# A two-block transformer kernel: SWA heads and MLA heads in one pipeline of single heads, gates as tanh

## The reference

```python
h = rmsnorm_2(x, mix_norm_g)
proj = h @ w_in          # 1024 x (512+128+128+384+256+32+1024+1024)
qa, ka, va, q_lat, kv_lat, k_r, g_a, g_b = split(proj)
qa, ka = rope(qa), rope(ka)                      # 8 query heads, 2 key heads of 64
o_a = swa_sink_attention(qa, ka, va, sinks)      # window of 128, a sink in the sum
cq = rmsnorm_2(q_lat, q_norm_g); qb = cq @ w_uq  # 384 -> 8 heads of 64+32
ckv = rmsnorm_2(kv_lat, kv_norm_g); kvb = ckv @ w_ukv   # 256 -> 8 x (64+64)
o_b = mla_attention(q_nope, rope(q_rope), k_nope, rope(k_r), vb)  # 8 causal heads
y = sigmoid(g_a) * (o_a @ w_o_swa) + sigmoid(g_b) * (o_b @ w_o_mla)
x = x + y @ w_out
```

## Time and profile before

| | |
|---|---|
| median of three runs | 1207.67 us |
| the profiled execution | 1208.16 us |
| its span, first to last instruction | 1206.3 us |
| PE busy / DVE busy / ACT busy | 1152.8 / 693.5 / 577.8 us |
| second mixer, from its second input piece to the first product with `w_out` | 823.9 to 984.9 us |
| PE clock in slices 31 and 33 of 40 | 0.9 |
| PE clock in slice 32 | 0.6 |

### The profile page before, as it was taken

The page is one execution under the profiler, slowest core; times in us unless marked ns, Lnnn a source line. Parts: engine busy times, 40 slices in busy tenths (PEclk is TensorE's granted clock), DMA queues, the critical chain, the costliest instruction groups (busy, mean ns, idle before and its releaser), DMA issues. The chain is left out here.

```text
span 1206.3 us, 14165 instructions
## 1 busy us (share of the span) xinstructions
PE 1152.8 (96%) x5890; PEld 968.2 (80%) x5890; DVE 693.5 (57%) x779; ACT 577.8 (48%) x821; POOL 28.6 (2%) x34
## 2 busy tenths in 40 slices
PE   5999999999999999999999999999999889999997
PEld 4888887999989977777778888878887677888886
DVE  4654545667666667777466445455756266654443
ACT  4533345445455455654355433455556344534343
POOL 0000000000011200000000000000000000000000
PEclk9999999899999999999999999999999699999999
DMA  9565554555543335345456665654633234665650
GB/s 316 193 202 179 189 195 144 179 175 175 177 138 115 131 105 192 108 139 190 140 176 207 190 194 178 202 166 142 198 118 104 70 105 158 200 201 174 195 189 35
DMA packets 129967, 198.59 MB, mean 165 GB/s; under 512 B 5584, under 2 KB 98640, under 8 KB 129648
## 3 DMA queue, kind: packets, MB, share of 16 engines
q1 hardware_dynamic: 128272, 190.75, 48.8%
q0 software_dynamic: 1632, 6.95, 1.5%
HBM read 196.63 MB, written 1.05 MB: 164 GB/s over the span
## 5 line engine op out<-in xcount | busy, mean ns | idle before, releaser
L889 DVE TENSOR_TENSOR WL<-RAW,WH 128x2048 fp32r<-128x2048 f32 (+1 forms) x181 | 405.7, 2264 | 104.3 <-ACT WH L429 104.1
L429 ACT ACTIVATE WH<-RAW 128x2048 fp32r<-128x2048 f32 (+1 forms) x181 | 338.3, 1890 | 18.8 <-DMA RAW<-in_w_in 9.4
L1435 PE MATMUL PS<-WH,XTH 128*128 128x512 f32 (+1 forms) x700 | 277.3, 396 | 1.4 <-ACT V L616 0.9
L1437 PE MATMUL PS<-WH,XTL 128*128 128x512 f32 (+1 forms) x700 | 273.1, 390 | 0.0
L1436 PE MATMUL PS<-WL,XTH 128*128 128x512 f32 (+1 forms) x700 | 272.4, 389 | 0.0
L1435 PE MATMUL ACC<-WH,KTH 128*128 128x512 f32 (+1 forms) x466 | 186.6, 400 | 9.3 <-DVE KTL L978 6.0
L1437 PE MATMUL ACC<-WH,KTL 128*128 128x512 f32 (+1 forms) x466 | 183.8, 395 | 0.0
L1436 PE MATMUL ACC<-WL,KTH 128*128 128x512 f32 (+1 forms) x466 | 183.7, 394 | 0.0
L1435 PEld LDWEIGHTS PS<-WH,XTH 128*128 128x128 f32 x700 | 131.5, 188 | 27.8 <-ACT V L616 1.4
L1437 PEld LDWEIGHTS PS<-WH,XTL 128*128 128x128 f32 x700 | 131.4, 188 | 27.9
L1436 PEld LDWEIGHTS PS<-WL,XTH 128*128 128x128 f32 x700 | 131.6, 188 | 25.8
(11 more groups left out here) (258 smaller groups left out, 1322.0 us busy)
## 6 DMA issues: line engine op xcount, KB each, us to landing
RAW<-in_w_in SPq DMA_DIRECT2D x48, 1024.0 KB, 5.2
RAW<-in_ffn_w_gate SPq DMA_DIRECT2D x44, 512.0 KB, 4.0
RAW<-in_ffn_w_up SPq DMA_DIRECT2D x44, 512.0 KB, 5.0
RAW<-in_ffn_w_down SPq DMA_DIRECT2D x22, 1024.0 KB, 4.9
RAW<-in_w_gate SPq DMA_DIRECT2D x22, 512.0 KB, 3.9
RAW<-in_w_up SPq DMA_DIRECT2D x22, 512.0 KB, 4.9
RAW<-in_w_down SPq DMA_DIRECT2D x11, 1024.0 KB, 4.9
RAW<-in_ssd_w_branch SPq DMA_DIRECT2D x8, 1024.0 KB, 5.0
```

Source lines behind the costliest of these rows:

```text
L429: nc.scalar.activation(WH[:, s, 0:n], RAW[:, s, 0:n], ACT.Copy).then_inc(w_hi, 1)
L889: tt(WL[:, s, 0:n], RAW[:, s, 0:n], WH[:, s, 0:n].bitcast(F32), ALU.subtract).then_inc(w_lo, 1)
L1435: mm(ps, stat_hi, mov_hi, start=first, stop=False)
L1437: return mm(ps, stat_lo, mov_hi, start=False, stop=last)
```

## The change

Only the second mixer changes.

- The input projection's pieces are cut otherwise (`IN2_COLS`): first the query latent and the SWA keys (512 columns), then the SWA queries (512), then SWA values, the KV latent and the rope key (416).
- The order of units is new: `U_UQ` at once after the projection, the gate chunks `U_G2` between and behind `U_UKV` and `U_OSWA`.
- The 16 heads (8 SWA, then 8 MLA) go singly through a loop of 18 steps. In step q PE computes the scores of head q, a `cover(q)`, the products with V of head q-2, the transposes of the probabilities of head q-1, and in steps 7 to 14 the four transposes of MLA head q-7. Scores have one PSUM bank (4), turned probabilities one (5), products with V one (6).
- A cover is a piece for one tile of 128 tokens: 12 matmuls of 512 columns in most steps, 24 in steps 0, 1, 10, 11 and 12. All gate chunks, `U_UKV`, the whole SWA branch (steps 11 and 12) and the first piece of the MLA branch (step 17) are covers.
- The gates are kept as tanh of half the logit, straight from PSUM (ACT's `g2_keep`). The merges compute (tanh + 1) times product in one instruction, and `kt_hi` and `kt_lo` of the product with `w_out` carry a factor 0.5. The sigmoid passes (L790) and their table load are gone; a load of the table set with exp and tanh is added ahead of the heads.

The core of the diff:

```diff
-            for q in range(1, 3):
-                banks = (in2_bank(q, 0), in2_bank(q, 1))
...
-            first_half(g2_unit(0), (0, 1), lambda t: pe.wait_ge(proj_kept, t + 3))
...
+            def head_scores(q):
+                r = q % SWA_HEADS
+                if q:
+                    pe.wait_ge(s2_ready, q)
+                if q < SWA_HEADS:
...
+                else:
+                    pe.wait_ge(mla_kept, r + 1)
+                    qt, kt = QK[0:MLA_QK, r, 0, :], QK[0:MLA_QK, r, 1, :]
+                mm(PS[4][:, 0:P], qt[:, 0:P], kt[:, 0:P], start=True, stop=True)
+                mm(PS[4][:, P:3 * P], qt[:, P:TOK], kt[:, :], start=True, stop=True).then_inc(sc2, 1)
+            def head_turn(q):
+                pe.wait_ge(p2_exp, q + 1)
+                if q:
+                    pe.wait_ge(p2_kept, q)
...
+            def head_values(q):
+                pe.wait_ge(p2_kept, q + 1)
+                if q:
+                    pe.wait_ge(o2_kept, q)
...
+            for q in range(18):
...
+                if q < 16:
+                    head_scores(q)
+                if 0 < q < 17:
+                    cover(q)
+                if q >= 2:
+                    head_values(q - 2)
+                if 1 <= q <= 16:
+                    head_turn(q - 1)
+                if 7 <= q <= 14:
+                    if q == 7:
+                        pe.wait_ge(kcat_ok, 1)
+                    elif q == 10:
+                        pe.wait_ge(k_lo, 17)
+                    elif q == 11:
+                        pe.wait_ge(k_lo, 18)
+                    turn_mla(q - 7)
```

On ACT:

```diff
+            for q in range(18):
+                if q < 16:
+                    head_exp(q)
+                if q == 0:
+                    split_hi()
+                elif q == 1:
+                    split_hi()
+                    g2_keep(0)
+                elif q == 2:
+                    split_hi()
+                    kv_keep(0)
+                elif q == 3:
+                    kv_keep(1)
+                elif q == 7:
+                    g2_keep(1)
+                elif q in (4, 6, 8, 12, 14, 15):
+                    split_hi()
+                elif q == 10:
+                    kt_hi(16, U_UKV + 1)
+                    g2_keep(2)
+                    split_hi()
+                elif q == 11:
+                    kt_hi(17, U_UQ + 2)
+                    split_hi()
...
+                if 1 <= q <= 16:
+                    act.wait_ge(p2_turned, q)
...
+                    nc.scalar.activation(PT2[(q - 1) % 2], PS[5][:, 0:384], ACT.Copy).then_inc(p2_kept, 1)
+                if 7 <= q <= 14:
+                    r = q - 7
                     act.wait_ge(mla_turned, r + 1)
                     nc.scalar.activation(QK[0:MLA_QK, r, :, :], PS[7][0:MLA_QK, :].rearrange("p (a t) -> p a t", a=2),
                                          ACT.Copy).then_inc(mla_kept, 1)
```

On DVE (`head_max` is the mask, the two maxima and the negative maximum; `head_out` the output of a head):

```diff
+            for q in range(18):
+                if q < 16:
+                    head_max(q)
+                if 1 <= q <= 16:
+                    head_sum(q - 1)
+                if q >= 2:
+                    head_out(q - 2)
+                if q == 0:
+                    query_rope()
+                    split_lo()
+                elif q == 3:
+                    key_cat()
+                elif q in (1, 2, 4, 6, 8, 14, 15):
+                    split_lo()
+                elif q == 10:
                     kt_lo(16)
                     split_lo()
+                elif q == 11:
+                    kt_lo(17)
+                    split_lo()
+                    branch_merge(0)
+                elif q == 12:
+                    split_lo()
+                    branch_merge(1)
+                elif q == 16:
+                    kt_lo(18)
```

More of the change, by code:

```diff
@@ L256, in program, with head_sm @@
         KDUP = REST[:, 0:512].rearrange("p (t j u c) -> p t j u c", t=NT, j=SWA_KV, u=2)
+        def head_sm(q):
+            n = 10 * (q % 3)
+            return [SM[:, n + 2 * k:n + 2 * k + 2] for k in range(5)]
         GPRE = SCR[:, 2048:3072]
@@ new lines, in head_exp @@
+            def head_exp(q):
+                act.wait_ge(s2_ready, q + 1)
+                mx, nmax, sums, sink, rec = head_sm(q)
+                r = q % SWA_HEADS
+                for i in range(NT):
+                    p = SC[q % 2][:, i * P:i * P + P * (i + 1)]
+                    ins = nc.scalar.activation(p, p, ACT.Exp, scale=(HD if q < SWA_HEADS else MLA_QK) ** -0.5,
+                                               bias=nmax[:, i:i + 1], accum_out=sums[:, i:i + 1])
+                    if i == 0:
+                        own.inc(ins)
+                if q < SWA_HEADS:
+                    own.inc(ins)
+                    ins = nc.scalar.activation(sink, nmax, ACT.Exp, bias=ROWS[:, ROW["sinks"] + r:ROW["sinks"] + r + 1])
+                ins.then_inc(p2_exp, 1)
@@ L1279, in _, with latent_scale, latent_lo @@
-            dve.wait_ge(swa_roped, 1)
+            def latent_scale(c0, rank, ss, n):
+                dve.wait_ge(lat_rs, n)
+                for t in range(NT):
+                    a = PROJ[:, t, c0:c0 + rank]
+                    ins = ts(a, a, RS[:, ss + t:ss + t + 1], None, ALU.mult)
+                    own.inc(ins) if t == 0 else ins.then_inc(lat_ok, 1)
+            def latent_lo(name, banks, first, last):
+                for j, (bank, k) in enumerate(banks):
+                    dve.wait_ge(lat_hi, first if j < 2 else last)
+                    ins = stt(KTL[:, j * TOK:(j + 1) * TOK], PS[bank][:, k * TOK:(k + 1) * TOK],
+                              COLS[:, GC[name] + j:GC[name] + j + 1], KTH[:, j * TOK:(j + 1) * TOK].bitcast(F32),
+                              ALU.mult, ALU.subtract)
+                ins.then_inc(lat_lo, 1)
@@ L1847, in _ @@
-            pe.wait_ge(g2_kept, 8)
-            pe.wait_ge(o2_kept, 8)
-            turn_rows(17, XN, 2)
-            for j in range(1, 4):
-                if j < 3:
-                    turn_rows(17 + j, XN, 2 * j + 2)
-                pe.wait_ge(k_lo, 17 + j)
-                rows(U_OSWA + j, j % 2 == 0, j % 2 == 1, half=j % 2, by_tile=(None, swa_half, None, branch_half)[j],
-                     tile_free=(lambda t: pe.wait_ge(acc_read, 6 + 2 * t)) if j == 2 else None)
-            by_pairs(20, U_OUT2, V, ready=lambda s: pe.wait_ge(merged, 4 + (1, 3, 2, 4)[s]))
+            turn_keys(6)
@@ L1858, in _ @@
+            cover(17)
+            pe.wait_ge(o2_kept, 16)
+            turn_rows(19, XN, 6)
+            mla_piece(0, 1)
+            pe.wait_ge(k_lo, 20)
+            mla_piece(1, 0)
+            mla_piece(1, 1)
+            by_pairs(20, U_OUT2, BUF2, ready=lambda s: pe.wait_ge(merged, 4 + (1, 3, 2, 4)[s]))
             norm(4, U_FFN3)
```

561 lines of the change are left out of this document (282 added, 279 removed).

## The result

The changed kernel takes 1210.59 us (median of 20 runs, 1208.81 to 1212.57), the kernel before 1207.75 us in the same batches (20 runs, 1204.62 to 1210.26). The ratio is 1.0025, 95% interval 1.0017 to 1.0032: 2.8 us slower, outside the interval of this many runs, and inside the 6 us that the forecast counted as no change. The forecast was 1214 us, 6.3 us slower, and it gave slower the largest chance, 0.47; no change had 0.30.

What follows compares the result with a forecast made beforehand. PE's own list and its waits were taken to bound the kernel. 114.7 us needed, 21.75 waits and 1.5 switches against 136.5, with 0.1 projection, gave +1.6; 1208.16 + 1.6 + 4.5 clock = 1214.3, stated as 1214 us, range 1199 to 1223.

Steps and rivals of the forecast that it cites:

- The work that is needed: Second mixer, projection's end to last branch product: PE needs 114.7 of the 136.5 us at 2.4 GHz.
- N: Stretch from first transpose of `norm(3, ...)` to the transpose behind the last branch product; forecast 176.95 us.
- the switches: PE changing between float32 and float32r some 16 times more, up to 0.11 us each: 1.5 us.
- The split chain: SWA steps with a split: maxima, exponentials, ACT's half, DVE's half follow each other, 6.75 us between heads' maxima.
- The MLA turns: Steps 8 to 15: scores wait for ACT's copy of transposes just issued, PE idling 0.85 us each, longer where ACT is late.
- the sum behind +1.6: Second mixer without clock falls: needed work, waits and switches make 137.95 us for 136.5, plus 0.1 from the projection.
- the clock term of 4.5 us: Second mixer: three falls of PE's clock after long waits, 1.5 us each with part hidden in the next wait.
- the waits of 21.75 us: PE's idle time: 9.2 us ahead of the heads and through step 6, 12.55 us from the MLA turns and step 17.
- The tail: The 3.00 us before the first product with `w_out`, where `kt_lo(20)` stands behind eight merge instructions, stay.
- A swinging clock: Rival: the clock falls in most steps, nine of sixteen losing 1.5 us; 1219 us, up to 1224; chance 0.2.
- PE setting the SWA steps: Rival: PE's 4.62 us, not the DVE and ACT chain, sets SWA steps; 1205.4, or 1199 to 1202 us; chance 0.27.
- Clock holds: Rival: no falls in the second mixer, the walk of waits alone, 1208 to 1212 us, no change; chance 0.08.

Runs made afterwards that it cites:

- Experiment 6: Changed kernel with ACT's split half last in its step, DVE's behind the next head's maxima, and MLA heads turned right behind the cover: 1193.53 us, ratio 0.9884.
- experiment 1: Changed kernel with ACT's half of the split ahead of the exponentials in steps 0 to 2: 1205.41 us, ratio 0.9974.
- experiment 10: Changed kernel with ACT's split half last in a step and DVE's behind the next head's maxima, MLA turn left late: 1203.23 us, ratio 0.9971.
- experiment 3: Changed kernel with a second PSUM bank for the scores of SWA heads 1, 3 and 5: 1208.71 us, ratio 1.0009.
- experiment 2: Changed kernel with MLA heads turned right behind the cover, their copy earlier on ACT, `kt_lo(16)` and `(17)` ahead of `head_out`: 1204.92 us, ratio 0.9974.
- experiment 5: Changed kernel with six useless 512-column matmuls in PE's wait of step 6: 1211.12 us, ratio 1.0027.
- experiment 9: Experiment 6 with `kt_lo(20)` moved ahead of the third product of `second_merge`: 1190.37 us, ratio 0.9865.
- experiment 4: Kernel before with only its gates changed to tanh, order of heads kept: 1206.45 us, ratio 0.9987.
- experiment 8: Changed kernel with the edits of experiments 1 and 2, and `kt_lo(20)` ahead of the third product of `second_merge`: 1197.12 us, ratio 0.9913.

## Why the prediction was wrong

**The work that is needed: right.** The forecast had 114.7 us from the projection's end on, so 149.1 us for N. Experiment 6, with no fall in N, has 154.39 - 4.94 = 149.45. That is right as a sum; its parts are less so, as said below under the switches.

**The split chain: right.** Masks 6.71 us apart for 6.75. The forecast maxima, moved by the 0.64 us by which this trace starts its norm earlier, are within 0.3 us of the traced ones for heads 0 to 6 (862.35, 869.14, 875.85, 882.57, 886.84, 893.56, 896.02, each mask's start and 1.47 us) and 0.5 us for head 7. Experiments 1 and 10 confirm the cause by taking it away, experiment 3 refutes the bank. Where PE sets the steps, in experiments 6 and 10, the masks of heads 2 to 7 are 4.7 to 4.8 us apart.

**The MLA turns: right in kind.** 0.77 us where 0.85 was forecast, and experiments 2, 6 and 10 show these waits shrink, go and stay with the order of the lists.

**The step that failed: the sum behind +1.6, that is the clock term of 4.5 us, and under it the waits of 21.75 us.** All of N:

| | forecast | measured |
|---|---|---|
| needed | 149.1 | 149.1 (taken over; experiment 6 has 149.45) |
| waits | 21.75 | 17.9 |
| clock | 4.5 | 3.4 (two falls of 1.7, of which 0.8 to 0.9 is missing from the waits) |
| the rest (switches in the forecast) | 1.5 | 2.4 |
| projection's cut | 0.1 | in the rest |
| N | 176.95 | 172.8 |

The clock fell twice in N and not three times, and one of the two stood ahead of a wait that ends by ACT (step 8), where it costs 0.8 us; net it cost about 2.5 us for 4.5. That is 2 us of the 4.1 that the forecast was over. I had looked for falls behind the waits of step 1, step 3, step 8 and steps 10 and 11. The changed kernel's first trace has one in step 6 and one in step 11, its second one in step 8 and one in step 11. Step 1 had none in either, though experiments 5, 9 and 10 fell right after the same 1.80 us; and the 2.99 us of the tail brought none in experiments 3, 4 and 5. So whether a given wait brings a fall is not settled by its length, and what settles it stays open.

The other 2 us are waits that I overpriced: 3.9 us too much, of which 0.9 went to the fall of step 6, less the 0.8 by which the rest is larger. By place, forecast against measured: ahead of the heads 1.4 and 1.27, step 1 1.9 and 1.80, steps 2 to 6 5.85 and 4.59, step 8 2.7 and 1.52 (2.28 in the execution without the fall ahead of it), the seven later copies 7.05 and 6.57, the turns behind `kt_lo` 1.55 and 1.29, step 17 1.25 and 0.82. In the SWA steps this is in part no error of the walk: DVE sets the step, so what PE's own work takes longer is missing from its wait and shows in the rest.

The walk without the clock gave +1.6 us and the trace shows +1.86. That agreement is luck: that sum left the clock out, and the net cost of the falls (2.5 us) and the overpriced waits (2.2 us with the rest) nearly cancel.

**The signs named beforehand.** From the projection's end to the last branch product it is 138.3 us (136 to 146 forecast), the 18 steps hold 16.6 us of idle time (under 12 would have meant wrong), and the clock is nowhere down for long: these came true. The "0.8 us or more before each MLA head's scores" did so for four of the eight; the other four are 0.77 or 0.78.

**Switches between float32 and float32r: too much as a sum, open one by one.** I took 1.5 us for them. Experiment 6 has all of them, and its rest is 0.35 us. But that is a net figure. From scores to scores PE takes 4.72 to 4.79 us there in steps 2 to 6, for 4.62 forecast, and 4.84 to 4.86 in steps 8, 9, 13 and 14, for 5.05. The forecast priced an MLA head's scores like an SWA head's 0.85 us; they take 0.52 (897.23 to 897.75 before). And the first matmul of a cover takes longer than the 0.23 us of the others, 0.33 behind an SWA head's scores and 0.42 behind an MLA head's, here in experiment 6:

```profile
875.89 0.50 PE L1473 MATMUL ACC<-WH,KTH 128*128 128x512 f32 x1
876.22 0.40 PE L1474 MATMUL ACC<-WL,KTH 128*128 128x512 f32 x1
...
904.69 0.58 PE L1473 MATMUL ACC<-WH,XTH 128*128 128x512 f32 x1
905.11 0.39 PE L1474 MATMUL ACC<-WL,XTH 128*128 128x512 f32 x1
```

So a price of about 0.1 us at a change is not refuted; the two errors cancel. The rest also shrinks with the number of idle starts: 2.4 us with 18, 1.8 with 13 in experiment 10, 0.35 with 3. It looks like about 0.13 us that each restart of PE costs beyond its wait; no run isolates that.

**Tanh at 0: supported.** Two kept gate pieces take 1.05 us, the plain copies 1.08, and experiment 4 is no slower.

**The tail: right.** 2.99 us as before; experiment 8 shows that it could have been cut to 1.67.

**The rivals.** A swinging clock: refuted. With 18 waits of 0.4 to 1.8 us the clock was at 1.00 in nearly all of N (two falls in the rows above). The rival's own sum is slightly off: nine times 1.5 us less a third is 9.0 and not 9.2 us. The Trainium skill (TensorE: Matmul & The Clock Gate, A second HAM failure mode) warns of a clock that swings all the time between groups of matmuls; no run here showed it. PE setting the SWA steps: refuted for this kernel, and it is what experiments 1, 6 and 10 made of it; experiment 1 gave 5.2 us where I had priced the waits at 5.85. Clock holds, 1208 to 1212: the right time, by another way.

The page on table loads (the Trainium skill, ScalarE: Activation LUTs, What ACT_TABLE_LOAD costs) speaks of a drain of 1.38 us beside the load. The added load shows none, as in the earlier trace rows: the next instruction starts 0.01 us after it, and the one ahead of it had ended at 846.42.

```profile
846.45 1.28 ACT L748 ACT_TABLE_LOAD   x1
847.74 1.92 ACT L434 ACTIVATE WH<-RAW 128x2048 fp32r<-128x2048 f32 x1
```

## What to carry to other kernels

Filling a stretch with dense work wins only if the small chains beside it keep up: here 21.8 us lost, most of it in one bad stretch, were exchanged for 18 waits and two falls. In an in-order list, place a piece that waits for another engine behind everything that a third engine wants soon, and put the producer's half a step earlier; the same instructions in another order were worth 17 us. Price a clock fall by what ends the step: in full (1.7 us here) only where PE itself does.

## What was not expected of the hardware

- The same kernel's clock fell at 895 in one execution and at 906 in the next, with the waits ahead of 893.60 equal to 0.02 us. Experiment 6 ran between 1191.89 and 1197.07 us, experiment 9, with a shorter wait at its end, within 0.33 us.
- Of the 21.8 us that the kernel before loses in its second mixer, 8.6 are idle and the rest, 13 us, clock: there the clock stayed down while small float32 work followed. In the changed kernel dense work follows soon behind each wait, and the clock was back after 3 to 4 us. That the work behind the wait makes this difference is argued, not shown.
- ACT's tanh from PSUM with a scale costs what its copy costs (1.05 and 1.08 us for two 128x512 pieces). DVE's (tanh + 1) times product in one instruction takes 1.28 us for two, the plain product of before 1.29; first experiment 4, then the kernel before:

```profile
975.29 1.28 DVE L1199 SCALAR_TENSOR_TENSOR SCR<-BUF,ACC 128x512 f32<-128x512 f32 x2 [4.63 <-PE ACC L1439]
...
978.91 1.29 DVE L1198 TENSOR_TENSOR SCR<-ACC,BUF 128x512 f32<-128x512 f32 x2 [4.73 <-PE ACC L1437]
```
